# Gather rings of 5 and 6 buffers in place of 7 and 8, in a one-core Hymba/PEER inference step

## The reference: what is computed

```python
e = take_along_axis(i1, ci // 16) * N_KEYS + take_along_axis(i2, ci % 16)   # 128 expert rows of each token
gate = softmax(top_s)
act  = gelu(einsum('thkd,td->thk', u_tab[e], hb))        # row of u_experts . token
out  = einsum('thk,thkd->td', gate * act, v_tab[e])      # weighted sum of rows of v_experts
```

## Time and profile before

| | |
|---|---|
| median of 3 runs | 3822.28 us (3820.02 to 3844.63) |
| the profiled execution, its own time | 3822.42 us |
| its span, first to last instruction | 3820.6 us |
| mean granted TensorE clock | 0.95 |
| DMA over the span | 1306 MB, 342 GB/s |
| first and last u gather of the prompt tiles | 316.5 and 3601.5 us |

### The profile page before, as it was taken

The page is one execution under the profiler, slowest core; times in us unless marked ns, Lnnn a source line. Parts: engine busy times, 40 slices in busy tenths (PEclk is TensorE's granted clock), DMA queues, the critical chain, the costliest instruction groups (busy, mean ns, idle before and its releaser), DMA issues.

```text
span 3820.6 us, 33128 instructions
## 1 busy us (share of the span) xinstructions
PE 3195.5 (84%) x10154; PEld 1603.0 (42%) x10154; DVE 2111.8 (55%) x5407; ACT 968.4 (25%) x2268; POOL 2516.1 (66%) x2183
## 2 busy tenths in 40 slices
PE   7975889998979888998889888988893878977577
PEld 6742345564325443553444333533351333443222
DVE  0118645655676547653766476647662376561943
ACT  1213322232223122321233123312231222321111
POOL 0005766777777758775877687777764687773575
PEclk9797999999999999999999999999996999988899
DMA  5347999999999999999999999999987999997698
GB/s 170 119 128 274 370 401 369 391 380 392 410 352 371 409 369 367 388 389 390 352 385 358 413 352 388 333 413 364 387 301 269 349 343 345 326 335 261 230 393 338
DMA packets 426704, 1306.16 MB, mean 342 GB/s; under 512 B 63090, under 2 KB 123794, under 8 KB 425378
## 3 DMA queue, kind: packets, MB, share of 16 engines
q0 software_dynamic: 313344, 1140.99, 78.9%
q1 hardware_dynamic: 113186, 163.06, 12.2%
HBM read 1286.61 MB, written 16.44 MB: 341 GB/s over the span
## 4 chain that ended last, share of the span: by engine, by line
PE 45%; DMA 23%; DVE 13%; POOL 11%; issue 5%; SPq 2%; ACT 2%; DVEq 0%; ACTq 0%; POOLq 0%
PE PS L885 23%; POOL R L528 10%; DMA R<-in_v_experts,idx 8%; PE PS L602 6%; DMA wring<-in_w_query 5%; DMA R<-in_u_experts,idx 5%; DMA wring<-in_w_out 5%; DVE R L1507 4%; PE PS L857 3%; PE PS L840 2%; PE PS L569 2%; PE PS L684 2%; SPq L313 2%; PE PS L683 2%; PE PS L665 2%
## 5 line engine op out<-in xcount | busy, mean ns | idle before, releaser
L885 PE MATMUL PS<-R,diag 128*128 128x512 f32 x4352 | 2093.5, 617 | 357.4 <-DMA R<-in_v_experts,idx 211.3
L1507 DVE CUSTOM_DVE_ANT_0 R<-R,hb 128x1024 f32<-128x1024 f32 x1088 | 1317.1, 1221 | 772.0 <-DMA R<-in_u_experts,idx 680.1
L528 POOL DMA_INDIRECT R<-in_u_experts,idx x1024 | 1188.0, 1160 | 721.7 <-DVE gate L1484 314.7
L528 POOL DMA_INDIRECT R<-in_v_experts,idx x1024 | 1196.1, 1168 | 511.6 <-PE PS L885 257.0
L885 PEld LDWEIGHTS PS<-R,diag 128*128 128x128 f32 x4352 | 795.9, 194 | 1414.3 <-issue 888.3
L1136 ACT ACTIVATE diag<-ident,w 128x128 f32<-128x128 f32 x1024 | 368.6, 392 | 621.6 <-PE PS L885 469.7
L602 PE MATMUL PS<-R 128*128 128x256 f32 (+1 forms) x1440 | 315.4, 375 | 0.9 <-DVE R L1199 0.9
L602 PEld LDWEIGHTS PS<-R 128*128 128x128 f32 x1440 | 268.2, 192 | 58.1 <-issue 24.3
L840 PE MATMUL PS<-wring,T 128*128 128x512 f32 x288 | 144.4, 626 | 110.8 <-DMA wring<-in_w_out 109.1
L857 PE MATMUL PS<-wring,T 128*128 128x512 f32 x288 | 148.0, 640 | 61.5 <-DMA wring<-in_w_query 60.1
L1140 ACT ACTIVATE acts<-dots 128x8 f32<-128x8 f32 x136 | 28.3, 208 | 591.3 <-DVE dots L1507 590.8
(11 more groups left out here) (210 smaller groups left out, 2324.3 us busy)
## 6 DMA issues: line engine op xcount, KB each, us to landing
R<-in_w_in SPq DMA_DIRECT2D x36, 1024.0 KB, 12.8
wring<-in_w_out SPq DMA_DIRECT2D x72, 512.0 KB, 6.7
wring<-in_w_query SPq DMA_DIRECT2D x72, 512.0 KB, 6.7
R<-in_u_experts,idx POOLq DMA_INDIRECT x1024, 7.0
R<-in_v_experts,idx POOLq DMA_INDIRECT x1024, 6.9
pr<-prd SPq DMA_DIRECT2D x8, 1232.0 KB, 8.5
prd<-stg SPq DMA_DIRECT2D x63, 128.0 KB, 5.8
xb<-in_x_prompt SPq DMA_DIRECT2D x8, 512.0 KB, 6.8
```

Source lines behind the costliest of these rows:

```text
L528: e.indirect_dma_start(dst, None, table, bass.IndirectOffsetOnAxis(ap=index, axis=0)).then_inc(S[s], c.count(name, s, 16))
L885: m = mm(bank(n), diag[:, s % DR, :], R[:, RU + s % RV, 512 * n:512 * n + 512], start=begins, stop=s == last_slot(t), skip_group_check=True)
L1507: e.tensor_tensor_reduce(R[:, g % RU, :], R[:, g % RU, :], hb[:, tile_of(g) % 2, :], 1.0, 0.0, ALU.mult, ALU.add, dots[:, g // GRP % 2, g ...
```

## The change

`RU` and `RV` become 5 and 6. `AUX` keeps its value 15, now written as a number, so all other users of `R` stay where they are and `R` keeps its 22 buffers. The u ring is now buffers 0 to 4, the v ring 5 to 10, and buffers 11 to 14 are used by nothing once the first projection pass is over. The base of that pass's chunks, which was `RU` = 7, is written as 7. Four semaphores go. No instruction is added, removed or moved on any engine: the waits of L551 and L556 now name the slots s - 5 and s - 6, and the landing waits name the semaphore of another buffer.

```diff
-RU, RV = 7, 8
-AUX = RU + RV
+RU, RV = 5, 6
+AUX = 15
 NR = AUX + 7
...
         def p_chunk(n, c):
-            i = RU + 2 * (c % 4) if n == 0 else AUX + 3 + 2 * (c % 2)
+            i = 7 + 2 * (c % 4) if n == 0 else AUX + 3 + 2 * (c % 2)
```

## The result

The changed kernel takes 3891.86 us (median of 4 runs, 3887.2 to 3906.27) against 3828.51 us for the kernel before beside it. The ratio is 1.0167, with a 95% interval of 1.0129 to 1.0205. On this chip the change costs 64 us, where the prediction had 90. The profiled execution took 3893.58 us, its span is 3891.8 us, 71.2 us longer than that of before.

A forecast was written before the change was run, and what follows sets the result against it. No single engine bounds throughout: PE in attention, transfers in weight stretches, POOL in quiet stretches. 18 stall ends x 5.0 us = 90 us on 3822.42 us gave 3912 us, own range 3867 to 3960, overall range 3830 to 4000.

The forecast's parts named there:

- The direction and the mechanism: Slower: where a consumer stalls, POOL stops two turns sooner and later cannot hide the four missing gathers; 90 us in all.
- The price of an end: Where a consumer's stall ends and POOL then bounds: two turns of POOL at 2.5 us each, 5.0 us lost.
- How many ends: Stall ends that cost: two in each of eight prompt tiles (attention, end of weight stretch), 16, plus 2 for tile 8.
- The two extra ends for tile 8: Two stall ends added for tile 8, where sample work sits and POOL waits for PE 18 times, for DVE 11.
- whose bound was 3997: Upper bound: all 27 POOL waits for DVE plus one deep PE wait per tile, 35 x 5.0 = 175 us.
- Nothing in the quiet stretches: Behind the weight stretches: no cost, since buffers are held 2.5 (u) and 2.9 (v) turns, fitting rings of 5 and 6.
- a share of DMA below 0.95: In the quiet stretches: a sign that the estimated buffer holding times were too short.
- The signposts: Profile signs expected: POOL's ring waits up over 90 us from 343, PE's v-row waits above 211, chunks landing after 6-7 us.
- The rule on the fixed cost of a gather: Gathers: about 2.0 us fixed plus bytes at 436 GB/s, about 3.2 us for 512 KB; by it the cost is 0.
- Faster: Weight chunks: fewer gathers in flight let them land sooner, 85 us gained less 15 lost, giving 3752 us; chance 0.06.
- Much slower: Attention stretches: short rings starve a consumer there too, 43 x 5.0 = 215 us, 3997 to 4040 us; chance 0.10.
- Its sign: Within attention: new idle time of PE waiting for v rows would mean that short rings starve a consumer there.

## Why the prediction was right, and where it was not

**The direction and the mechanism.** Right, on the first chip and, with half v rows, on the second. POOL's long waits stand two turns sooner in the tile, and most of the loss lies right behind the weight stretches, where POOL is full.

**The price of an end.** I took 2 x 2.5 = 5.0 us, and the last quarters of the eight tiles lost 5.3 us each on average. The match is closer than the reasoning was. The 2.5 us are the least that a turn costs POOL. In the quiet stretch, where POOL is full, my own row has 33 gathers in 50 us, 3.0 us a turn or 6.1 us for two. In tiles 2 to 7 the last quarters lost 37.3 us, 6.2 us each, which fits this price. Tiles 1 and 8 lost 3.5 and 1.8 us.

**How many ends.** This is the term that was too large. I took 18 ends at 5.0 us, 90 us. Measured were 71.7 us in 16 stretches, 4.5 us each: 42.6 us behind the weight stretches and 29.1 us in attention. That PE, at 125 of 125 us, covers part of the early stops in attention is my reading of the lower figure there, and no run takes it apart. The two extra ends for tile 8 do not show: its quarters sum to -1.1 us, though POOL waits there many times. Nor is every end a weight chunk's transfer, as I had counted: the deepest of them, tile 7's, is SP's late issue. Hence 3892 us where 3912 were forecast, inside the forecast's own range of 3867 to 3960. Part of that closeness is luck. The kernel before ran at 3828.51 us beside the change where the sum started from 3822.42, so the cost missed by 26 us of 90, the price a little too low and the count too high. The upper end of the own range, 3960, came from no term of the sum, whose bound was 3997.

**Nothing in the quiet stretches.** Right: POOL is full there before and after, the third window of both. The sign that I had named for the contrary, a share of DMA below 0.95, was badly chosen, since the row before already had 0.94. After the change it is 0.96.

**The signposts.** I expected POOL's ring waits to rise by more than 90 us, the rest being a shift. They rose by 71, with no shift in the sum. The place did shift, by two turns. The waits for DVE should have grown to several times 27, and grew to 42. PE's waits for v rows rose as said, from 211 to 269 us. PE's busy time should have stayed near 3195 us and grew to 3230. The chunks' landing stayed at 6.7 us.

**The rule on the fixed cost of a gather** ("DMA: Bandwidth & Descriptors" of the Trainium skill, section "Anatomy of one DMA — SWDGE (gpsimd) path") would have made the change free by my estimate from it. On the first two chips it did not, and the shortest landing after the change, 4.1 us, is again above the 3.2 us of that estimate. On the other two chips the change is free, but not because 11 buffers are ample: there the gain of the shorter v ring (44 to 64 us) and the loss of the shorter u ring (50 to 69 us) cancel.

**The rivals.** "Faster" did not act on the first chip. On two others the shorter v ring gained as much as the shorter u ring lost, and up to half of that may be this rival's mechanism, to which I gave 0.06. It had also counted the 55.4 us of tile 7 among the waits that a shorter queue could shorten, which SP's late issue rules out. "Much slower" did not come: in tile 4's attention PE stayed at 123.65 of 125 us. Its sign came in small, 1.3 us of waits for v rows there, and 74 in place of 53 us over all the attention quarters.

**What stays open.** Whether the u ring alone pays the 64 us on the first chip, since no single ring was timed there. How much of the 64 us would be left without tile 7's one long wait. What the shorter v ring gains on the slower chips, beyond the part that goes with PE's waits for chunks, and why only there. The 7 and 6 kernel was 1.1% faster than both kernels on two chips and was not run on the first, so it is no recommendation yet.

## What to carry to other kernels

In this kernel the mean time that a buffer is held said that 5 and 6 buffers would do, and the stalls said otherwise. So size a ring by the turns of lead that the producer must have when a consumer stalls. On the first two chips a shorter pair of rings cost about the producer's own time for the missing turns at each stall behind which the producer is the bound, and less where a consumer was fully busy. Take the producer's time for a turn from a stretch in which it is full, not from its shortest turn. Before counting a wait for a transfer as a matter of transfers, look when the transfer was issued. With two rings fed by one in-order queue, look at which wait holds the queue before giving both more: two v buffers more gained nothing on two of the four chips and cost 1.1% to 1.6%, and on the other two they were not tried alone. A difference of 1 to 2% should be timed on more than one chip before it is believed.

## What the runs showed of the hardware

- A quarter of the gathered bytes taken away, at the same number of gathers, saved 19 us of 3839, although the DMA engines had been busy for 0.99 of the stretch from 450 to 2700 us. With half v rows the share still reads 0.88 at 298 GB/s, so the share of busy DMA was no measure of what was left to gain here.
- The same kernel took 3829 and 3839 us on two chips and 4020 and 4022 us on two others, at a mean granted clock of about 0.950 and 0.925. Gathers took POOL about the same there (1.156 us on average for v with 5 and 6, 1.172 on the first chip), but by the profiles signals between engines came up to 12.06 us late.
- A change of 1.7% on the first chip was 0.1% on one of the slower two.
- With v rows of 2 KB beside u rows of 4 KB, gathers landed after 5.2 us at the median in place of 6.8 us, and took the DMA engines 15% less time for 25% fewer bytes (67.7% of 3802 us against 78.9% of 3821 us).
